# Stick-breaking attention: the gate projection dealt by whole groups of 24 matmuls in every second step

## The chip, the cores and the metric

One core of a Trainium2 chip. The metric is the device time of one execution of the whole program, in microseconds (us). The engines are TensorE (PE in the rows; PEld is its weight load), VectorE (DVE), ScalarE (ACT), GpSimd (POOL) and SyncE (SP), which issues the DMAs. Each engine works through its own instruction stream in order and waits on semaphores for the others.

## The reference

Two transformer-like blocks, batch 1, 1024 tokens, width 1024, float32. The first block runs a gated delta rule (branch a) and a stick-breaking attention (branch b) side by side and merges them through sigmoid gates; the second has latent and differential attention and a convolutional feed-forward. The edit concerns the stick-breaking attention and the gates:

```python
def _stick_breaking(q, k, v):              # 8 heads of 64
    scale = d ** -0.5
    for blk in range(s // SB_BLOCK):       # 8 tiles of 128 query rows
        z = einsum('bhqd,bhkd->bhqk', q[:, :, q0:end], k[:, :, :end]) * scale
        mask = kj < qi
        log_keep = where(mask, log_sigmoid(-z), 0.0)
        rest = cumsum(log_keep, axis=3, reverse=True) - log_keep
        a = where(mask, exp(log_sigmoid(z) + rest), 0.0)
        outs.append(einsum('bhqk,bhkd->bhqd', a, v[:, :, :end]))
...
gates = sigmoid(proj[..., B_Z1:G1] + b_gate)          # 2048 columns
merged = gates[..., :D_MODEL] * y_a + gates[..., D_MODEL:] * y_b
```

The matrix products with float32 inputs are done as three products of rounded parts (hi x hi, lo x hi, hi x lo).

## The kernel before

The program is a row of stages ("phases"). In each, several pieces of work ("stages" in the code) are written as generators, one for each engine, and a list, the plan, says which generator is advanced next. `run_stages` walks the same plan on every engine, so the plan fixes the order of the instructions in each of the five streams. The stage at hand is the phase `stick`, with three pieces in the plan: 0 is `StickAttention`, 1 is `GateProjection`, 2 is `BranchGates`.

**StickAttention** has 64 units: 8 tiles j of 128 query rows, by 8 heads h. A unit of tile j looks at j + 1 blocks of 128 keys. It runs as a software pipeline of 68 steps; step i holds, for unit i (tile i // 8, head i % 8):

- TensorE: in the first four steps of a tile four transposes of the next tile's prepared heads (`prep.turn`, L249) into a slot of `t`; the scores of unit i into `z` (L452 to L454); the products of unit i-3 with V into `o_acc` (`apply`, L476); the transposes of unit i-2's weights (`flip`, L463) into `t`. `t` has two slots, which head transposes and weight transposes take in turn.
- ScalarE: the high part of the transposed heads (`keep_hi`, L259), two sigmoids of the scores (`keep` L378, `chance` L381), in step 4 of a tile the squares for tile j + 2 (L213), then the copy of unit i-2's transposed weights out of the slot (L391).
- VectorE: the low part of the heads (`keep_lo`, L272 or L275), which frees their slot; the reversed scan of unit i (L426); in step 4 the sums for tile j + 2 (L219) and in step 7 their scaling (L239); the weights of unit i-1 (`weigh`, L402); and in step 2 of a tile `give` (L408), which multiplies the finished tile's `o_acc` into `stick_o`. The first products of a tile, in its step 3, wait for `give` (`pe.wait_ge(self.o_out, j)`), for they write `o_acc` anew.
- SyncE: loads of the prepared inputs and stores of `stick_o`.

**GateProjection** makes the gates' logits, transposed: 16 tiles of 128 gate columns, each in two halves of 512 tokens, that is 32 groups. A group is 24 matmuls of 128x512 (8 blocks of the inner dimension, three products each) into the one bank `g_acc`, and then one sigmoid by ScalarE (L567) and one store. `walk()` cuts each group in two parts of 12 matmuls, and `steps()` is 4 x 16 + 1 = 65. ScalarE and VectorE split the weights of the next tile into hi and lo (L554, L573) in the first part of a tile's second half; the first tile is split before the first part. SyncE stores the group before and loads weights for the next tile.

**BranchGates** takes eight steps a tile: a norm of branch a's output on GpSimd (L684 to L691, step 1), multiplications with the sigmoid gate (L696, L699, step 3), and the gate of branch b (L704, step 6), with loads and stores by SyncE.

The plan of the phase is `even_plan(68, 65)`: for each of the 68 steps it writes one step of StickAttention, one of BranchGates, and then as many of GateProjection as are due.

Of the kernel before, what the change touches and what calls it, by code (L numbers as in the profile page):

```python
# [710 lines left out]
def even_plan(first, second):  # L711


    plan, given = [], 0
    for i in range(first):
        plan += [0, 2]
        want = second * (i + 1) // first
        plan += [1] * (want - given)
        given = want
    return plan  # L720


# [3893 lines left out]
```

## Time and profile before

| | |
|---|---|
| median of 3 runs | 2792.08 us (2791.32 to 2796.21) |
| profiled execution, its time | 2794.54 us |
| profiled execution, its span | 2792.8 us |
| TensorE busy | 2614.5 us, 94% of the span |
| VectorE busy | 1263.7 us, 45% |
| ScalarE busy | 938.2 us, 34% |
| GpSimd busy | 357.3 us, 13% |
| mean granted TensorE clock | 0.967 of full speed |

The span is counted from the first to the last instruction on the core; the device time lies 1.7 us above it. Busy time says how long an engine had an instruction in hand. In rows of the timeline the first number is the start in us from the span's start, the second the duration in us, "x3" that three neighbours of the same line are merged, and a bracket at the end how long the engine sat idle before the row and who released it. Matmul durations overlap: the next one starts before the modelled end of the one before, so distances between starts are read, not durations.

### The profile page before, as it was taken

What the parts mean: (1) busy time and instruction counts of PE and PEld (TensorE: products, weight loads), DVE (VectorE), ACT (ScalarE), POOL (GpSimd) and SP (SyncE); (2) the same over time, 40 slices, a digit from 0 to 9 for tenths busy, and PEclk for the clock granted to TensorE, in tenths of its full rate; (3) what the DMA queues carried; (4) which work ended last, traced back from release to release, by engine and by line L of the source; (5) the groups of instructions that cost most, each with busy time, mean ns of one, the idle gap of its engine ahead of it and who ended that gap; (6) DMA issues with size and microseconds to landing.
All of it is one profiled execution on the core that took longest, in us unless ns stands there. A gap on an engine that the chain in (4) does not pass through costs nothing. (4 is left out here: it accounts for less than half of the span.)

```text
span 2792.8 us, 36573 instructions
## 1 busy us (share of the span) xinstructions
PE 2614.5 (94%) x14702; PEld 2246.8 (80%) x14702; DVE 1263.7 (45%) x1762; ACT 938.2 (34%) x1541; POOL 357.3 (13%) x450
## 2 busy tenths in 40 slices
PE   8969999997799998999996989979999999999999
PEld 6849999997688886888885777868888888878877
DVE  6523444442466754543225767554323332333452
ACT  4223222221455652122114767532111211222331
POOL 1002222220332310001012223011000000000000
PEclk9989999999799998999997999989999999999999
DMA  4222221112332215442343111063222222255532
GB/s 144 86 77 80 62 68 52 52 41 68 106 113 88 80 50 192 155 143 82 121 135 119 46 39 47 18 222 89 83 68 68 68 83 76 91 189 176 192 102 80
DMA packets 223712, 268.91 MB, mean 96 GB/s; under 512 B 55060, under 2 KB 154004, under 8 KB 223544
## 3 DMA queue, kind: packets, MB, share of 16 engines
q1 hardware_dynamic: 223544, 266.58, 30.0%
q8 instruction: 117, 1.92, 0.3%
q14 instruction: 51, 0.42, 0.0%
HBM read 187.21 MB, written 79.32 MB: 95 GB/s over the span
## 5 line engine op out<-in xcount | busy, mean ns | idle before, releaser
L3784 PE MATMUL ffn_up_acc<-mixed_hi,ffn_ring_hi 128*128 128x512 f32 x704 | 274.6, 390 | 2.5 <-DVE mixed_lo L2926 2.5
L3784 PE MATMUL ffn_up_acc<-mixed_hi,ffn_ring_lo 128*128 128x512 f32 x704 | 274.3, 390 | 0.0
L3784 PE MATMUL ffn_up_acc<-mixed_lo,ffn_ring_hi 128*128 128x512 f32 x704 | 274.2, 389 | 0.0
L1379 PE MATMUL delta_acc<-delta_w_hi,xn_hi 128*128 128x256 f32 x640 | 191.6, 299 | 2.9 <-DVE delta_w_lo L1333 2.9
L1381 PE MATMUL delta_acc<-delta_w_hi,xn_lo 128*128 128x256 f32 x640 | 181.3, 283 | 0.0
L1380 PE MATMUL delta_acc<-delta_w_lo,xn_hi 128*128 128x256 f32 x640 | 181.1, 283 | 0.0
L3784 PEld LDWEIGHTS ffn_up_acc<-mixed_hi,ffn_ring_hi 128*128 128x128 f32 x704 | 132.2, 188 | 30.0 <-issue 2.9
L3784 PEld LDWEIGHTS ffn_up_acc<-mixed_hi,ffn_ring_lo 128*128 128x128 f32 x704 | 132.2, 188 | 27.5
L3784 PEld LDWEIGHTS ffn_up_acc<-mixed_lo,ffn_ring_hi 128*128 128x128 f32 x704 | 132.3, 188 | 27.1
L4043 DVE TENSOR_TENSOR ffn_feed_lo<-ffn_feed_raw,ffn_feed_hi 128x1536 fp32r<-128x1536 f32 x44 | 77.4, 1759 | 146.2 <-ACT ffn_feed_hi L4035 146.2
L3754 DVE TENSOR_SCALAR ffn_conv<-ffn_padded,ffn_taps 128x1024 f32<-128x1024 f32 x22 | 16.6, 753 | 274.8 <-ACT ffn_padded L3735 274.8
L1379 PEld LDWEIGHTS delta_acc<-delta_w_hi,xn_hi 128*128 128x128 f32 x640 | 122.2, 191 | 8.9 <-issue 5.5
L426 DVE TENSOR_TENSOR_SCAN stick_keep<-stick_keep,stick_zero 128x127 f32<-128x127 f32 (+7 forms) x64 | 92.4, 1444 | 74.1 <-ACT stick_keep L378 73.4
L3735 ACT ACTIVATE ffn_padded<-ffn_up_acc 128x1024 f32<-128x1024 f32 x22 | 22.6, 1027 | 301.4 <-PE ffn_up_acc L3784 301.4
L1380 PEld LDWEIGHTS delta_acc<-delta_w_lo,xn_hi 128*128 128x128 f32 x640 | 122.2, 191 | 0.0
L1381 PEld LDWEIGHTS delta_acc<-delta_w_hi,xn_lo 128*128 128x128 f32 x640 | 121.9, 191 | 0.0
L4035 ACT ACTIVATE ffn_feed_hi<-ffn_feed_raw 128x1536 fp32r<-128x1536 f32 x44 | 65.4, 1487 | 158.9 <-PE ffn_up_acc L4111 158.9
L593 PE MATMUL stick_g_acc<-xn_hi,stick_g_hi 128*128 128x512 f32 x256 | 107.8, 421 | 9.3 <-DVE stick_g_lo L573 8.8
L4111 PE MATMUL ffn_up_acc<-ffn_feed_hi 128*128 128x512 f32 x352 | 108.7, 390 | 1.4 <-DVE ffn_emb L3897 1.4
L4111 PE MATMUL ffn_up_acc<-ffn_feed_hi,ffn_feed_lo 128*128 128x512 f32 x352 | 108.5, 390 | 0.0
L4111 PE MATMUL ffn_up_acc<-ffn_feed_lo,ffn_feed_hi 128*128 128x512 f32 x352 | 108.4, 390 | 0.0
L594 PE MATMUL stick_g_acc<-xn_lo,stick_g_hi 128*128 128x512 f32 x256 | 102.0, 399 | 0.0
(440 smaller groups left out, 6462.3 us busy)
## 6 DMA issues: line engine op xcount, KB each, us to landing
ffn_feed_raw<-in_w_down SPq DMA_DIRECT2D x44, 512.0 KB, 4.0
ffn_ring_raw<-in_w_gate SPq DMA_DIRECT2D x11, 1024.0 KB, 5.3
ffn_ring_raw<-in_w_up SPq DMA_DIRECT2D x11, 1024.0 KB, 5.8
scratch_act_t<-ffn_silu SPq DMA_DIRECT2D x22, 512.0 KB, 2.7
ffn_feed_raw<-scratch_act_t SPq DMA_DIRECT2D x44, 256.0 KB, 2.9
delta_w_raw<-in_w_in SPq DMA_DIRECT2D x20, 512.0 KB, 4.0
scratch_projected<-delta_out SPq DMA_DIRECT2D x80, 128.0 KB, 1.7
stick_g_raw<-in_w_in SPq DMA_DIRECT2D x16, 512.0 KB, 4.7
```

Source lines behind the costliest of these rows:

```text
L426: nc.vector.tensor_tensor_scan(back, back, self.zero[:].to_broadcast([P, n - 1]), 1.0, ALU.mult, ALU.add).then_inc(self.scanned, 1)
L593: nc.tensor.matmul(self.acc[:], w_hi, self.hi[:, k, cols], start=(k == 0), stop=False, skip_group_check=True)
L594: nc.tensor.matmul(self.acc[:], w_hi, self.lo[:, k, cols], start=False, stop=False, skip_group_check=True)
L1379: nc.tensor.matmul(acc, self.hi[:, k, tok], w_hi, start=(k == 0), stop=False, skip_group_check=True)
L1380: nc.tensor.matmul(acc, self.hi[:, k, tok], w_lo, start=False, stop=False, skip_group_check=True)
L1381: last = nc.tensor.matmul(acc, self.lo[:, k, tok], w_hi, start=False, stop=(k == self.kt - 1), skip_group_check=True)
L3735: nc.scalar.activation(self.padded[s][:, taps - 1:], self.acc[s][:, 0, :], ACT.Copy).then_inc(self.copied, 1)
L3754: nc.vector.tensor_scalar(self.conv[s][:], self.padded[s][:, 0:SEQ], self.taps_sb[:, f, 0:1], None, ALU.mult).then_inc(self.tapped, 1)
L3784: last = nc.tensor.matmul(self.acc[s][:, br, cols], weight[:, k, ch], part[:, k, cols], start=(k == 0 and first), stop=(k == 7 and weight ...
L4035: self.nc.scalar.activation(self.hi[s][:], self.raw[s][:], ACT.Copy).then_inc(self.hi_done[s], 1)
L4043: self.nc.vector.tensor_tensor(self.lo[s][:], self.raw[s][:], self.hi[s][:].bitcast(F32), ALU.subtract).then_inc(self.lo_done[s], 1)
L4111: last = nc.tensor.matmul(t.pairs[j][:, half, :], part, weight[:, HALF + half * HALF:HALF + (half + 1) * HALF], start=begins, stop=ends, s ...
```

## The change

`even_plan` gives the gate steps out only behind odd steps, and there an even number of them; the last step gets what is left. Everything else is as it was.

```diff
@@ -714,9 +714,10 @@
     plan, given = [], 0
     for i in range(first):
         plan += [0, 2]
-        want = second * (i + 1) // first
-        plan += [1] * (want - given)
-        given = want
+        if i % 2 or i == first - 1:
+            want = second * (i + 1) // first if i == first - 1 else second * (i + 1) // first // 2 * 2
+            plan += [1] * (want - given)
+            given = want
     return plan
```

## Rows read from the trace of the kernel before

**Rows 1.** TensorE by windows: length, busy (instructions), granted clock, DMA share, GB/s

```profile
727.00:1055.00 328.00, 324.60 (x1974) 1.00 0.28 86
1630.00:1640.00 10.00, 8.47 (x55) 1.00 0.23 62
1650.00:1660.00 10.00, 7.40 (x58) 0.92 0.01 2
```

**Rows 2.** Waits of TensorE, 727 to 1056: total us, times, longest

```profile
PE stick_o_acc L476 <- DVE stick_o L408: 2.4, 4, 1.1
PE stick_g_acc L593 <- ACT stick_gate L567: 0.4, 2, 0.3
```

**Rows 3.** Timeline of steps 21 to 23: start, us, engine, line, instruction, [idle before]

```profile
803.21 0.34 PE L452 MATMUL stick_z<-stick_prep_k,stick_prep_q_hi 128*128 128x384 f32 x1
...
807.42 0.34 PE L452 MATMUL stick_z<-stick_prep_k,stick_prep_q_hi 128*128 128x384 f32 x1
...
807.83 0.83 PE L476 MATMUL stick_o_acc<-stick_v,stick_weight_t 128*128 128x64 f32 x6
...
808.75 0.42 PE L452 MATMUL stick_z<-stick_prep_k,stick_prep_q_hi 128*128 128x384 f32 x1
...
809.03 0.49 ACT L391 ACTIVATE stick_weight_t<-stick_t 128x384 f32<-128x384 f32 x1
...
809.57 0.88 PE L476 MATMUL stick_o_acc<-stick_v,stick_weight_t 128*128 128x64 f32 x6 [0.17 <-ACT stick_weight_t L391]
```

**Rows 4.** Timeline of step 2 in tiles 1, 3 and 7

```profile
757.55 0.38 PE L476 MATMUL stick_o_acc<-stick_v,stick_weight_t 128*128 128x64 f32 x2
...
761.11 0.69 DVE L408 TENSOR_TENSOR stick_o<-stick_o,stick_o_acc 128x512 f32<-128x512 f32 x1
...
823.92 0.83 PE L476 MATMUL stick_o_acc<-stick_v,stick_weight_t 128*128 128x64 f32 x6
...
825.18 1.30 POOL L691 TENSOR_TENSOR stick_a_o<-stick_a_o,stick_a_gain 128x512 f32<-128x512 f32 x1
825.25 2.31 DVE L426 TENSOR_TENSOR_SCAN stick_keep<-stick_keep,stick_zero 128x511 f32<-128x511 f32 x1
...
827.48 1.70 DVE L402 TENSOR_TENSOR stick_chance<-stick_chance,stick_keep 128x511 f32<-128x511 f32 x1
...
829.21 0.69 DVE L408 TENSOR_TENSOR stick_o<-stick_o,stick_o_acc 128x512 f32<-128x512 f32 x1
...
830.04 1.08 PE L476 MATMUL stick_o_acc<-stick_v,stick_weight_t 128*128 128x64 f32 x8 [1.10 <-DVE stick_o L408]
...
1002.46 1.72 PE L476 MATMUL stick_o_acc<-stick_v,stick_weight_t 128*128 128x64 f32 x14
...
1007.94 0.69 DVE L408 TENSOR_TENSOR stick_o<-stick_o,stick_o_acc 128x512 f32<-128x512 f32 x1
```

**Rows 5.** Timeline of step 4 in tile 3

```profile
834.73 1.05 PE L476 MATMUL stick_o_acc<-stick_v,stick_weight_t 128*128 128x64 f32 x8
...
835.61 1.22 DVE L426 TENSOR_TENSOR_SCAN stick_keep<-stick_keep,stick_zero 128x511 f32<-128x511 f32 x1 [3.09 <-ACT stick_keep L378]
...
836.89 0.61 ACT L391 ACTIVATE stick_weight_t<-stick_t 128x512 f32<-128x512 f32 x1
...
838.18 0.68 DVE L402 TENSOR_TENSOR stick_chance<-stick_chance,stick_keep 128x511 f32<-128x511 f32 x1
```

**Rows 6.** Timeline of step 0 in tile 1

```profile
749.77 0.38 PE L476 MATMUL stick_o_acc<-stick_v,stick_weight_t 128*128 128x64 f32 x2
...
750.39 0.75 DVE L272 SCALAR_TENSOR_TENSOR stick_prep_q_lo<-stick_t,stick_prep_gain,stick_prep_q_hi 128x512 fp32r<-128x512 f32 x1 [0.17 <-ACT stick_prep_q_hi L259]
```

**Rows 7.** Timeline of the first gate split

```profile
720.00 1.85 DVE L573 TENSOR_TENSOR stick_g_lo<-stick_g_raw,stick_g_hi 128x1024 fp32r<-128x1024 f32 x1 [1.83 <-ACT stick_g_hi L554]
```

**Rows 8.** Timeline of step 64, near the stage's end

```profile
1041.78 1.04 PE L463 MATMUL stick_t<-ident,stick_chance 128*128 128x128 f32 x8
1042.43 1.08 ACT L391 ACTIVATE stick_weight_t<-stick_t 128x512 f32<-128x512 f32 x2 [4.33 <-PE stick_t L463]
```

## The prediction

> **What bounds the kernel now.** I read the page's slices first, then the stage that the edit orders (the attention stage with the stick-breaking heads, about 690 to 1060 us), by windows, by TensorE's waits, and then row by row in time. From 727 to 1055 us TensorE is busy 324.6 of 328 us at a granted clock of 1.00 [rows 1]. Its named waits there are 2.4 us for VectorE's `stick_o` in four places and 0.4 us for the gate's activation [rows 2]. So TensorE's own instruction stream is the stage. Neither side of the edit changes the number of matmuls, so nothing can be gained in the steady part beyond those few microseconds; what can be lost is the cover that the gate matmuls give to the chain ScalarE, VectorE, TensorE of the attention.
>
> How cover works shows where the plan before has a step without gate work, step 22 (tile 2, three key blocks). A step with 12 gate matmuls takes 807.42 - 803.21 = 4.21 us, step 22 only 808.75 - 807.42 = 1.33, so a half group is worth 2.88 us of TensorE. In step 23 the products with V start at 809.57 and not right behind the scores (about 809.24): they need ScalarE's copy of the transposed weights, 809.03 + 0.49 = 809.52 [rows 3]. One uncovered step cost 0.33 us, of which the trace names less.
>
> **What the change does.** `even_plan(68, 65)` gave one gate step (12 matmuls) to each stick step but 0, 22 and 45. Worked out by its formula, it now gives none to even steps and two (24 matmuls, 5.76 us) to steps 3, 5, ... 43 and 47 ... 65, none to 45, and the last three (a group and the final store) to step 67. No instruction is added or removed. In each pair (even a, odd a+1) TensorE runs scores, products and transposes of two steps in a row and only then 24 gate matmuls. Let S be the end of the scores of step a. Cover behind step a+1 is ample. What is late is what step a+1 needs from step a: the slot of `t` for its own head transposes, the copied weights of unit a-2 for the products, and VectorE's weights of unit a-1 for the transposes. For step 22 S is 807.83, and TensorE is ready for the next products 1.41 us later (809.24) at three key blocks: 808.75 - 807.83 = 0.92 for products and transposes, 0.31 a block, and 0.49 for the scores [rows 3]. I scale the first by the blocks, take 0.4 to 1.0 for the scores, and about 0.36 for head transposes where they lie between.
>
> *Pair (2,3) of tiles 1 to 7.* The products of step 3 (head 0) write `stick_o_acc` and wait until `give` has read it; `give` is VectorE's last instruction of step 2, behind keep_lo, the scan and the weights. From S to the end of `give` it is 761.80 - 757.55 = 4.25 us in tile 1, 829.90 - 823.92 = 5.98 in tile 3, and 1008.63 - 1002.46 = 6.17 in tile 7; the products follow 0.14 us behind [rows 4]. In tile 3 they started at 830.04 with 1.10 us of wait, so TensorE's work up to there was 5.02 us, 2.14 without the gate's 2.88. The wait becomes 5.98 + 0.14 - 2.14 = 4.0 us; in the same way, by the rate above, 3.1 in tile 1 and 2.9 in tile 7. Seven of 3.3 are 23 us: the upper bound. But scan and weights ran beside GpSimd's multiplies there: the scan took 2.31 us [rows 4], against 1.22 for the same shape in rows 5, and the weights 1.70 against 0.68. Without this tile 3 waits 1.9, and all seven about 14: the lower bound. GpSimd's work starts in step 1 and step 2 now comes 2.88 us later, but its last multiply needs step 2's sigmoid, so part of it still meets the scan. I take 20.
>
> The Trainium skill (GPSIMD Engine Reference, section 1, Specifications) says that GpSimd shares its SBUF interfaces with VectorE and contends with VectorE instructions that have two SBUF inputs. The scan of these rows agrees (2.31 beside a multiply, 1.22 alone); going by that rule for every one of the seven tiles would give the upper bound of 23.
>
> *Pair (4,5) of tiles 0 to 5.* In step 4 ScalarE squares the inputs of a later tile ahead of the copy, and VectorE sums them ahead of the weights. In tile 3, S = 834.73: the copy ends at 837.50, 2.8 later; the weights at 838.86, 4.1 later [rows 5]. TensorE is at the products at about 1.9 (four blocks and the scores), waits 0.9, spends 0.9 on them, and waits 0.5 more for the weights: 1.4. The same reading gives 2.2, 2.05, 1.7 (tiles 0 to 2) and 1.1, 0.6 (4, 5): 9.1, and with the gate's activation now ahead of every even step's first sigmoid in small tiles 9.5 us.
>
> *Pair (0,1) of tiles 1 to 6.* Step 1's head transposes need the slot of step 0's. In tile 1, S = 749.77 and keep_lo ends at 751.14 [rows 6]; with 0.05 of hand-over and about 0.15 for that activation it is 1.57 against 0.33 us of TensorE work: 1.2 us. In tiles 2 to 6 it is 0.8, 0.35, 0.05, 0.7, 0.65 (in the last two the slot is freed by the copy), with some 0.3 behind it: 4.1 us.
>
> *The rest.* Pairs with nothing extra, (6,7) mostly, by rows 3: 0.33 us at three blocks, more for shorter and less for longer units, 2.8 in all. Three steps in a row without cover (44 to 46): 0.3. At the end, step 65's products need the copy of unit 62: the transposes start at 1041.78 and the copies end at 1043.51 [rows 8]; eight transposes keep TensorE until about 1042.7: 0.9. At the start the gate's first split moves from step 1 to step 3 in ScalarE's and VectorE's order. It ended at 721.85 [rows 7]; behind steps 2 and 3 I put it near 724.5, some 2.7 later, while about 2.1 us of TensorE work of those steps moves into the wait: 0.6 (from -2 to +2). SP's loads keep their place, since nothing that SP waits for lies in steps 1 to 3; the gate's weight loads and stores are still issued a whole pair ahead of use.
>
> Sum of new waits: 20 + 9.5 + 4.1 + 2.8 + 0.3 + 0.9 + 0.6 = 38.2 us. What goes: the 2.8 us of rows 2, the 0.33 of step 22, and some 0.9 of like waits at step 45 and before head-0 transposes (steps 7, 15 ... now have double cover): 4.0. Net +34 us on the profiled execution (span 2792.8, 2794.5 with what lies around it), all of it in this stage; the same on the median of 2792.1: **2826 us**. The waits are not made good later, since TensorE has no slack in this stage, and the next stage starts from its last matmul: the last gate activation leads to the last two stores and those to the next stage's loads, in the same order as before.
>
> **Rivals.**
> *Only the bare uncovered step costs* (0.13). If `give` and the sums end by the time TensorE gets there, because ScalarE and VectorE enter step a with empty queues after 5.76 us of cover, each of the 31 pairs costs what step 22 did: 31 x 0.33 = 10, less 4: +6 to +12, 2801. Against it: rows 4 and 5 measure from S, behind which the chain starts afresh whatever the cover was.
> *The clock falls too* (0.07). TensorE now stops for 1 to 4 us in every pair. Rows 1 show 8.47 us busy of 10 at clock 1.00 with a wait in it, and 7.40 of 10 at 0.92; the worst pairs here, tiles 0 to 2, are busy some 75 to 80%. A group of 24 at half clock costs up to 5.8 us more; four to six of them make +57 to +69: 2855. The Trainium skill (TensorE: Matmul & The Clock Gate, "A second HAM failure mode") says that frequent short idling between groups can make the clock swing between its two levels; by that rule this rival would be the likeliest. The first of these rows speaks against it, the second for it.
> *Faster* (0.05). The long groups of 24 and the long weight-load wait at the head absorb the chains: the 4.0 us of old waits go, 2.1 us of steps 2 and 3 run while TensorE waited anyway, and the split isn't late. That is -6 us, 2786. It decides only if the chain from S is no longer than TensorE's work in the even step; at 4.25 against 1.3 us in tile 1 it is not.
> *No net change* (0.05): the waits come, but small, and match what is refunded: 2792, within 5.6 us.
>
> **Numbers.** The forecast has 0.70, its own range 2814 to 2838 (23 or 14 for `give`, half of the smaller terms either way). Slower in all: 0.70 + 0.13 + 0.07 = 0.90. A change is told from none at 0.2%, 5.6 us. The range reaches into the first rival below and to the upper bounds of all terms above: 2800 to 2843.
>
> **What would show it.** In the changed profile: TensorE's busy share of the stage falls from 99% to about 90%; a wait for `stick_o` in seven places, 2 to 4 us each; waits of the transposes for `stick_chance` and of the products for `stick_weight_t` in steps 5 of tiles 0 to 5; waits of step 1's head transposes; clock at 1.00; the stage's last gate activation some 34 us later than now; all stages behind as long as before. I would be wrong if the `stick_o` waits stay near 1 us, if GpSimd's multiplies have ended by every step 2, if the clock drops, or if TensorE's queue reaches past a waiting matmul.

## The result, and the profile after

The changed kernel takes 2841.68 us (median of 4 runs, 2836.43 to 2844.21) against 2791.7 (4 runs, 2790.81 to 2796.21): ratio 1.0174, 95% interval 1.0161 to 1.0187, so 1.7% slower, some 49 us. The forecast was 2826 in a range of 2800 to 2843; the direction and the place were right, the loss was nearly half as large again (49 us against 34).

The profiled execution took 2836.43 us with a span of 2834.7, 41.9 longer. I call the stretch from the attention's first sum on VectorE to the next stage's first load of `gated` the stage: it was 370.4 us (689.8 to 1060.2) and is 415.9 (689.0 to 1104.9), +45.5. Everything else went from 2422.4 to 2418.8. So the whole loss is in this stage.

TensorE by windows, as [rows 1] before (length, busy, granted clock, DMA share, GB/s), the second a stop in tile 2, the others in 1 us steps behind it:

```profile
727.00:1097.00 370.00, 336.80 (x1950) 0.97 0.25 76
804.00:806.00 2.00, 0.00 (x0) 1.00 0.68 203
...
807.00:808.00 1.00, 1.00 (x7) 0.58 0.48 178
808.00:809.00 1.00, 1.00 (x6) 0.50 0.97 182
...
810.00:811.00 1.00, 1.00 (x4) 0.72 0.29 98
811.00:812.00 1.00, 1.00 (x6) 1.00 0.00 0
```

Two things can be seen. TensorE is idle 33.2 us of 370, where it was 3.4 of 328. And the granted clock isn't 1.00 any more: behind the stop it goes to 0.50, the lower level of 1.2 GHz, with TensorE fully busy, and comes back near 811. Added up over 1 us windows as 2 x (1 - clock), the time at the lower level between 727 us and the last gate activation is 0 before and 22.1 us after.

TensorE's waits in the stage, as [rows 2] before:

```profile
PE stick_o_acc L476 <- DVE stick_o L408: 16.9, 7, 3.3
PE stick_o_acc L476 <- ACT stick_weight_t L391: 7.7, 11, 1.4
PE stick_t L463 <- DVE stick_chance L402: 2.5, 5, 0.9
PE stick_t L249 <- ACT stick_weight_t L391: 2.5, 5, 0.6
PE stick_t L249 <- DVE stick_prep_q_lo L272: 1.9, 3, 1.1
PE stick_t L249 <- DVE stick_prep_k L275: 1.5, 2, 1.0
```

Seven waits for `give` (VectorE L408), the copies (ScalarE L391), the weights (`stick_chance`, L402) and the slot of the head transposes (L249): the places that the forecast named. Tile 3, steps 2 and 3, answers to [rows 4]:

```profile
845.08 0.83 PE L476 MATMUL stick_o_acc<-stick_v,stick_weight_t 128*128 128x64 f32 x6
...
846.40 2.04 DVE L426 TENSOR_TENSOR_SCAN stick_keep<-stick_keep,stick_zero 128x511 f32<-128x511 f32 x1
...
847.70 1.80 POOL L699 TENSOR_TENSOR stick_a_o<-stick_a_o,stick_a_sig 128x512 f32<-128x512 f32 x1 [0.33 <-ACT stick_a_sig L657]
...
848.37 1.68 DVE L402 TENSOR_TENSOR stick_chance<-stick_chance,stick_keep 128x511 f32<-128x511 f32 x1
...
850.08 0.69 DVE L408 TENSOR_TENSOR stick_o<-stick_o,stick_o_acc 128x512 f32<-128x512 f32 x1
...
850.92 0.52 PE L476 MATMUL stick_o_acc<-stick_v,stick_weight_t 128*128 128x64 f32 x3 [3.31 <-DVE stick_o L408]
```

Step 2's products start at S = 845.08. Scan, weights and `give` follow one another without a gap, and end 5.69 us later (5.98 before); the products of step 3 wait 3.31 us for them (1.10 before). Scan and weights still run beside GpSimd's multiplies: 2.04 and 1.68 us.

### The profile page after: what moved, and what is told of

It reads as the page before. It is cut to its first block and busy times, and to the rows that moved or that the text cites. A ratio compares the mean times of both kernels' runs of the same rounds, so it can differ in the third digit from the quotient of the medians.

```text
span 2834.7 us, 36573 instructions
## 1 busy us (share of the span) xinstructions
PE 2625.7 (93%) x14702; PEld 2253.5 (79%) x14702; DVE 1258.6 (44%) x1762; ACT 936.4 (33%) x1541; POOL 349.7 (12%) x450
## 3 DMA queue, kind: packets, MB, share of 16 engines
q1 hardware_dynamic: 223544, 266.58, 29.7%
## 5 line engine op out<-in xcount | busy, mean ns | idle before, releaser
L3785 PEld LDWEIGHTS ffn_up_acc<-mixed_lo,ffn_ring_hi 128*128 128x128 f32 x704 | 132.7, 188 | 27.3
```

What stands on the lines that cost most here:

```text
L3785: last = nc.tensor.matmul(self.acc[s][:, br, cols], weight[:, k, ch], part[:, k, cols], start=(k == 0 and first), stop=(k == 7 and weight ...
```

## The experiments

The first column of the table is the ratio to the kernel before with its 95% interval. The others are from one profiled execution each: the stage's length less before's 370.4; TensorE's idle time and the time at the lower clock level, both from 727 us to the last gate activation. In e5 the last group comes some steps before the stage's end, so that its idle column lacks the drain, the steps 64 to 67 in which the pipeline empties (10.7 us up to 1066 us). The profiled execution is the shortest of its kernel in the change, e1, e3 and e6 and the longest in e2, e5 and e7, so the stage's column and the ratio can differ by some us.

| | ratio (95%) | stage, us | idle, us | lower clock, us |
|---|---|---|---|---|
| before | | 0 | 3.5 | 0 |
| the change | 1.0174 (1.0161 to 1.0187) | +45.5 | 33.2 | 22.1 |
| e1, step 2 alone | 1.0134 (1.0117 to 1.0150) | +38.3 | 24.5 | 34.2 |
| e2, step 4 alone | 1.0038 (1.0025 to 1.0051) | +11.6 | 13.0 | 0 |
| e3, steps 0 and 6 alone | 1.0048 (1.0034 to 1.0061) | +14.5 | 14.7 | 0 |
| e4, even steps | 1.0156 (1.0143 to 1.0169) | +44.3 | 27.3 | 38.3 |
| e5, steps 1, 2, 4, 7 | 1.0036 (1.0022 to 1.0050) | +12.0 | 9.8 | 0.9 |
| e6, change and fillers | 1.0131 (1.0114 to 1.0148) | +39.0 | 16.7 | 4.7 |
| e7, change, give first | 1.0097 (1.0083 to 1.0111) | +31.2 | 24.1 | 9.7 |
| e8, before, give first | 0.9989 (0.9980 to 0.9997) | -3.2 | 1.2 | 0 |
| e9, e5 with other last places | 1.0046 (1.0032 to 1.0060) | +13.2 | 11.5 | 0 |

Theory A is the forecast's mechanism with the clock added: a step pays for the chain that loses its cover, and where TensorE stops long the clock falls as well. Its rivals are C, all uncovered steps cost the same; D, groups of 24 matmuls in a row, or half of the steps without gate work, cost in themselves; and B, the clock costs nothing.

**One kind of step at a time (e1, e2, e3).**

```diff
         want = second * (i + 1) // first
+        if i % 8 == 2 and i > 8:          # e1
+        if i % 8 == 4 and i < 48:         # e2
+        if i % 8 in (0, 6) and i > 2:     # e3
+            want = given
         plan += [1] * (want - given)
```

Each kernel has one of the three conditions. That of e1 also meets step 66 of the drain, where its trace shows no wait.

e1 expected: 

> The plan of before, but the gate step of step 2 of tiles 1 to 7 is given behind step 3 instead (24 matmuls there). Theory A (each pair pays for the chain that it uncovers, and the clock falls where TensorE stops longest): the waits for stick_o rise from 2.4 to about 17 us in seven places, and in about five of them the granted clock falls for some 3.4 us, which costs 1.7 us each; +14.5 + 8.5 = about +23 us. Theory B (only the waits cost, the clock is a side effect): +14.5. Rival C (every uncovered step costs the same, what step 22 costs): seven times 0.33, +2.3 us, no more.

e2 expected: 

> The plan of before, but the gate step of step 4 of tiles 0 to 5 is given behind step 5. Theory A: the copy of the weights and the weights themselves come late behind the squares and sums; TensorE waits about 2.2, 1.9, 1.5, 1.1, 0.7, 0.6 = 8 us, and the clock falls at most once (tile 0): +8 to +10 us. Rival C: six times 0.33, +2 us.

e3 expected: 

> The plan of before, but the gate steps of steps 0 and 6 of each tile (from step 6 on) are given behind steps 1 and 7. Theory A: the head transposes of step 1 wait for their slot, 2.9 us over six tiles, the products of step 7 for the copy, about 1.1 us, less what waits before step 0's head transposes go; clock 1.00 throughout: +3 to +4 us. With e1 and e2 it should add up to the change, about +37 of its +50, the rest being the first two steps, the end and the clock. Rival C: fifteen times 0.33, +5 us.

Waits of TensorE in the stage, e1:

```profile
PE stick_o_acc L476 <- DVE stick_o L408: 17.6, 7, 3.6
...
PE stick_g_acc L593 <- ACT stick_gate L567: 3.7, 6, 0.9
```

e2:

```profile
PE stick_o_acc L476 <- ACT stick_weight_t L391: 5.2, 7, 1.0
PE stick_g_acc L593 <- ACT stick_gate L567: 2.8, 4, 0.9
...
PE stick_t L463 <- DVE stick_chance L402: 2.2, 4, 0.8
```

e3:

```profile
PE stick_g_acc L593 <- ACT stick_gate L567: 8.5, 11, 0.9
...
PE stick_t L249 <- DVE stick_prep_q_lo L272: 1.6, 3, 0.9
PE stick_o_acc L476 <- ACT stick_weight_t L391: 1.3, 4, 0.8
```

C falls: seven steps of kind 2 cost 37 us, six of kind 4 cost 11, fifteen of kinds 0 and 6 cost 13. e1 shows the `give` waits as expected (17.6 us in seven places), but cost 37 us and not 23. The clock was low for 34.2 us, twice what was expected, for it fell behind all seven; and idle time grew by 21.0 us where 14.5 were expected, with waits for the gate's sigmoid and for head transposes on top. The sum nearly closes: idle +21.0, half of 34.2 is 17.1, together 38.1 against the stage's 38.3. Half is what rows at either level give, roughly: in the changed kernel the starts of two gate matmuls lie 0.43 us apart at the lower level (725.14 and 725.56) and 0.23 at the upper (1099.50 and 1099.73).

All three hold a wait that the change has not: the first matmul of a group for the gate's sigmoid, 3.7, 2.8 and 8.5 us. I had not foreseen it, and it is why e3 missed its expectation of 3 to 4 us (e2, with 8 to 10 expected, came near). Less this wait e3's fifteen steps cost some 5 us, 0.35 each, which is what step 22 cost and what C had said for them; it is the steps of kinds 2 and 4 that C has wrong. Steps before the doubled one hand out one half group each, so 24 matmuls in a row can be the second half of one group and the first half of the next, with the sigmoid of 0.69 us between, and there is only the one bank `g_acc`. The change deals whole groups and has none. Less these waits (15.0, and 0.4 of before's in each) the three cost 61.4 - 13.8 = 47.6 us in all; the change costs 48.6. That the two agree to 1 us is partly luck, for the falls of the clock don't add.

**Whole groups behind even steps (e4).**

```diff
-        if i % 2 or i == first - 1:
+        if i % 2 == 0 or i == first - 1:
```

> Whole groups of 24 as in the change, but behind even steps. Theory A: what decides is which chain the uncovered (odd) step starts. The waits for stick_o go back to below 1 us and those behind squares and sums vanish; in their place the head transposes of step 0 wait for VectorE's scaling of step 7 (2.27 us long, ahead of it sigmoid and scan), some 2.5 to 3 us in each of seven tiles, +18 to +20, the slots in step 2 some 4, the rest 3; with the clock falling in up to seven places (1.7 us each) +30 to +38 us. Theory D (24 matmuls in a row are themselves what costs, or the longer idle of ScalarE): the same +50 as the change. Rival E (only step 2 and 4 are expensive): within 5 us of before.

Waits in e4:

```profile
PE stick_t L249 <- DVE stick_prep_xn L239: 17.0, 6, 3.0
PE stick_o_acc L476 <- ACT stick_weight_t L391: 4.3, 11, 0.8
```

The `stick_o` waits are gone from the list and those for `stick_prep_xn`, VectorE's scaling in step 7, are new: 17.0 us in six places, up to 3.0. Another chain gave the same price. The ratio can't be told from the change's, so e4 alone leaves D standing. Idle is less than in the change (27.3), the lower clock longer (38.3): half of it, 19.1, and 23.8 of added idle are 42.9 of the stage's +44.3. Rival E, that only steps 2 and 4 matter, falls, and 44 us is more than the 30 to 38 that I had expected, by the clock.

**Whole groups behind steps 1, 2, 4 and 7 (e5), and with other last places (e9).**

```diff
-        want = second * (i + 1) // first
+        due = sum(k % 8 in (1, 2, 4, 7) for k in range(1, i + 1))                                            # e5
+        due = sum(k % 8 in (1, 2, 4, 7) and k < 56 or k in (58, 62, 65, 66) for k in range(1, i + 1))        # e9
+        want = second if i == first - 1 else min(2 * due, second - 1)      # e5; in e9 2 * due, which never exceeds second - 1
         plan += [1] * (want - given)
```

e5 expected: 

> Whole groups of 24 as in the change, but behind steps 1, 2, 4 and 7 of each tile, so that give (step 2), squares and sums (step 4) and the scaling (step 7) are covered and the cheap steps 0, 3, 5 and 6 are not; steps 64 to 66 have no cover. Theory A: left are the slot of the head transposes (2.9 us), the copies behind steps 3, 5 and 6 (some 5 us) and the drain at the end (2.5), less 4 us of old waits: idle about 14 us against 33 in the change, no wait long enough for the clock to fall: +5 to +12 us. Theory D (groups of 24, or that half of the steps have no gate work, are what costs): near the change's +50.

e9 expected: 

> As e5, but the last four groups stand behind steps 58, 62, 65 and 66, so that the drain of the pipeline is covered; steps 59 to 61 and 63 and 64 of tile 7 are not, where eight key blocks keep TensorE long enough. Theory A: e5's stage ended 13.3 us later than before's; the three waits in the drain (1.5, 0.8, 0.8 as idle time before the copies and products, and the last product with nothing behind it) go, and the stage ends 7 to 9 us later than before's: +4 to +9 us. Theory D (a gap between e5 and before is due to groups of 24 in themselves): no better than e5, +10.

Waits in e5:

```profile
PE stick_o_acc L476 <- ACT stick_weight_t L391: 4.6, 13, 0.8
PE stick_t L463 <- DVE stick_chance L402: 3.4, 7, 0.9
...
PE stick_t L249 <- DVE stick_prep_q_lo L272: 1.9, 3, 1.1
PE stick_t L249 <- ACT stick_weight_t L391: 1.0, 2, 0.6
```

The same 32 groups of 24, half of the steps still without gate work, and a loss of 10 us in place of 49. D falls as the cause of the 49 us. No wait for `give`, sums or scaling is left, the longest of the rest is 1.1 us, and the clock stays (the 0.9 us in the table are at 727 us, the end of the low stretch with which the stage begins). e9 missed its expectation of 4 to 9 us with 13: the drain itself was covered, but steps 63 and 64, which now had no gate work, brought two waits of 0.8 us for the copies, and nothing was won. That is what D had said for e9, no better than e5, and a small D isn't excluded: of the stages' +12.0 and +13.2 us, idle time and clock explain about 7 and 8, and the other 5 are taken up behind the forecast's terms.

**What the clock costs (e6).**

```diff
             if 0 <= i - self.LAG - 1 < len(self.units):
+                gate, count = self.gate, 8 * (i % 8 == 3 and 8 < i < 64) + 4 * (i % 8 == 5 and i < 44)
+                if count:
+                    pe.wait_ge(gate.gated, (i - 3) // 2 - (i > 45))
+                    for _ in range(count):
+                        nc.tensor.matmul(gate.acc[:], c["ident_r"][:], gate.hi[:, 0, 0:HALF], start=True, stop=True,
+                                         skip_group_check=True)
                 apply(i - self.LAG - 1)
...
+                stick.gate = gate
```

> The change, with 8 matmuls of 128x512 that nothing uses put ahead of the products of step 3 (tiles 1 to 7) and 4 ahead of those of step 5 (tiles 0 to 4), where TensorE waits anyway. It leaves the waited-for instructions where they are. Theory A with the clock as a cost of its own: half-clock time of 22 us goes to about 0 and TensorE's idle time falls by some 16 us; the time falls by half of the half-clock time, 8 to 11 us, to about +40 us against before. Theory B (the clock costs nothing, because the half-clock stretches are refunded by later waits): the time stays at +50. If the fillers delay the products themselves, +51 to +55.

Waits in e6:

```profile
PE stick_o_acc L476 <- DVE stick_o L408: 4.8, 6, 1.5
PE stick_o_acc L476 <- ACT stick_weight_t L391: 3.1, 8, 0.8
```

With 76 matmuls more, some 18 us of TensorE work, the kernel is faster than the change: ratio 1.0131 with an interval that ends at 1.0148, where the change's begins at 1.0161; that is +37 us where about +40 was expected. TensorE's low-clock time goes from 22.1 to 4.7 us, half of the difference is 8.7, and the stage is 6.5 shorter; in tile 6, where the wait was 0.86 us, the eight fillers are longer than what they fill. B falls: the clock's share is a loss of its own. In tile 3 the clock fell even so (847 to 851 us), behind a wait of 1.47 us that the fillers had left.

**give ahead of the scan, in the change (e7) and in the kernel before (e8).**

```diff
+                u = i - self.LAG - 1
+                if 0 <= u and self.units[u][1] == H - 1:
+                    give(self.units[u][0])
                 dve.wait_ge(self.kept, i + 1)
                 back = self.keep[b][:, n - 1:0:-1]
...
-            if 0 <= u < len(self.units) and self.units[u][1] == H - 1:
+            if i >= len(self.units) and 0 <= u < len(self.units) and self.units[u][1] == H - 1:
                 give(self.units[u][0])
...
-        want = second * (i + 1) // first                                    # e8 only, in even_plan
+        want = second if i == first - 1 else i - (i >= 60) - (i >= 62)      # e8 only
```

e7 expected: 

> The change, with VectorE's give moved ahead of the scan in step 2 of each tile. Theory A (give is late because it stands behind scan and weights): the waits for stick_o fall from 16.9 to about 3 us; scan and weights come 0.6 to 1.2 us later, so step 3's transposes wait 0.5 to 2 us instead, 8 us in all; half the clock falls go: 12 to 20 us less than the change, +30 to +38 against before. Rival: the products wait for something else as late as give (copy, slot), and nothing is won.

e8 expected: 

> The plan of before with give ahead of the scan, and with the two stick steps without gate work moved from 22 and 45 to 60 and 62, where eight key blocks cover the copy. Theory A: 2.4 us of waits for stick_o and about 0.6 us at the two steps go: -1 to -3 us, which the measurement hardly tells from nothing. Rival: the scan that comes later costs as much elsewhere, 0 to +2 us.

Waits in e7, whose lines stand three further down (L463 is L466, L476 is L479):

```profile
PE stick_t L466 <- DVE stick_chance L402: 9.9, 12, 1.6
PE stick_o_acc L479 <- ACT stick_weight_t L391: 7.7, 11, 1.4
```

The 16.9 us of waits for `stick_o` are gone, while the transposes wait 9.9 us for the weights (2.5 in the change), for scan and weights now come later; low-clock time falls to 9.7. The result, +27 us, is 22 better than the change and a little better than the 30 to 38 expected: it was `give`'s place at the end of VectorE's step 2 that made step 2 the dearest. In the kernel before the same edit, with the two steps without gate work moved to 60 and 62 (tile 7, eight key blocks), leaves 1.2 us of idle in place of 3.5 and gives 0.9989 (0.9980 to 0.9997): some 3 us faster than before, as expected, and the fastest of all here. By the trace most of it is `give`: the four waits for it are gone and one of 0.35 us for the weights is new, while step 22's wait was 0.17; by time the two edits weren't told apart.

## Why the prediction was right, and where it was short

*What bounds the stage, and the sign.* Right: TensorE had 3.4 us of idle, nothing was to be won there, and covers were to be lost. e5, with the groups placed by the chains, loses 10 us.

*Pair (2,3), give, 20 us.* Right. In the change the waits for `give` are 16.9 us in seven places; in the same pairs the head transposes of step 3 wait first, 2.9 us in five places, which my sum from S held inside the 20. Together 19.8, by tile (1 to 7) 3.6, 3.4, 3.3, 3.2, 3.0, 1.2 and 2.2. That 20 was met so closely is partly luck, for the split by tile is another: the upper bound had 4.0 in tile 3 and 2.9 in tile 7. Between the two bounds (14 and 23) the meeting with GpSimd went as taken: beside the multiplies the scan took 2.04 us and the weights 1.68 in tile 3, against 1.22 and 0.68 in [rows 5]. In tile 6 the scan ran between two multiplies, and the wait for `give` was 0.86. What the meeting costs rests on these rows; no run takes the multiplies away.

*Pair (4,5), 9.5 us.* Measured by tile 2.2, 1.9, 1.5, 1.1, 0.7, 0.6, in all 8.0, against 2.2, 2.05, 1.7, 1.4, 1.1, 0.6. *Pair (0,1), 4.1:* 2.9. *The rest, 2.8:* 1.1 named by the trace; as in step 22 it names less than the rows show. *Steps 44 to 46, 0.3:* 0.28. *The end, 0.9:* 0.83. *The start, 0.6:* the first gate matmul comes at 724.12, not 721.90; counted from the stage's own start (689.03, not 689.81) that is 3.0 later, with about 2 us of TensorE work moved ahead of it, so some 1 us. All waits together are 33.2 us of idle against 3.5, +29.7; the forecast had +34.

*The clock.* Here the forecast fell short. "The clock falls too" stood beside the forecast as a rival with 0.07, so that it was no term of the sum, and was priced at four to six groups run wholly at the lower level. What happened is the forecast's waits and the clock: it fell behind the five stops of 2.5 to 3.3 us (tiles 1 to 5) and behind tile 0's 1.38 and 0.85 us within 2 us of each other, not behind the 2.18 us of tile 7 nor the 0.86 of tile 6; 22.1 us at the lower level, which cost half of it, 11. (Of the 22.1, 1.6 at 727 to 729 us are the end of the low stretch with which the stage begins.)

The rows that I weighed it by were windows of 10 us with 8.5 and 7.4 us busy, and I read them by their busy time alone. The second holds more when it is taken in steps of 1 us: TensorE stood still for 1.84 us up to 1657.27, and one us later, while it was busy, the granted clock went to 0.72 and then to 0.50, where it stayed to about 1665, through a second stop of 1.84 us before 1661.19. So the trace of the kernel before already held a fall of the clock behind a stop shorter than those that the forecast itself put into seven tiles. Seen so, there was reason to make the clock a term of the sum and not a rival with 0.07; its price of four to six groups (23 to 35 us) would have been too high, for it cost 11. The first window had stops of 0.39 and 1.13 us, at a clock of 1.00.

Of the page of the Trainium skill that I cited (TensorE: Matmul & The Clock Gate, "A second HAM failure mode") the trace shows the swing between the two levels. Here it came behind single long stops, or two stops close together, and not behind frequent short ones: e2, e3, e5 and e9 have about twenty waits each, of up to 1.1 us, and no fall behind any of them. In between it isn't settled: in e7, where no wait is longer than 1.62 us, the clock fell twice, behind 1.37 and 0.85 us in tile 0 and behind 1.04 us and a shorter one in tile 2, and not behind the 1.62; in e6 it fell behind 1.47.

*The rest, and the range.* The sum then reads +29.7 of idle and +11.0 of clock, 40.7 of the stage's +45.5. Counted over the whole stage up to the last gate activation's end it is the same: TensorE is idle 57.8 us against 29.3, and busy at the lower level for 24.2 us more, which makes 28.5 and 12.1, together 40.6. So the other 4.9 lie neither in idle time nor in the clock but inside TensorE's busy time, with 2016 matmuls both times; waits that hide behind the modelled ends of matmuls would be counted there. The same rest is 4.9 us in e5 and 5.1 in e9, and 1.5 in e1, which leaves only seven steps more without gate work. An estimate from step 22 would be enough for it: there the trace named 0.17 us of 0.33, and 0.16 for each of 31 uncovered steps is 5.0. No run tests it, and it is the part of rivals C and D that stays open.

That 2842 lies inside the stated range is partly luck. The upper end, 2843, was made of larger waits; the waits came out smaller than the sum had them, and the clock and this rest, for neither of which the sum had a term, filled the gap. Of the signs named beforehand, TensorE's busy share (91% of the window) and the places of the waits came as said; the last gate activation came 44.7 us later and not 34; and "if the clock drops", which stood among the signs of being wrong, came too.

The profiled run was the fastest of the four (2836.4 us; the others 2840 to 2844). Their mean granted clocks are 0.966, 0.965, 0.964 and 0.964 in the order of their times: 0.002 less over 2840 us is 11 us more at the lower level, 6 us of time. More falls of the clock in the other three would fit, but no profile of them was taken.

## What to carry to other kernels

Work dealt out as cover between the steps of a chain is worth what the step behind it would wait, and the steps differ: here taking 12 matmuls away cost 0 to 1 us behind most steps, 1 to 2 behind those with squares and sums (e2), and about 5, with the clock that fell after it, behind the one whose last VectorE instruction the next products wait for (37 us for seven in e1). Before covers are bunched, follow each kind of step from a common point to the last thing that the next step needs, on each engine in its program order; and if they must be bunched, put them where these chains are longest, and cut them at the boundaries of their own accumulation. When the sum leaves TensorE standing for some us at a stretch, look in the trace at hand for stops of that length, in steps of 1 us, and see whether the granted clock fell behind them; if it did, add half of the time at the lower level as a term of its own, not as a rival.

## What the runs showed of the hardware

Useless matmuls in a wait of 2.5 to 3.3 us made a kernel faster than the same kernel without them (1.0131 against 1.0174): 76 of them took about as much time as the idle time that went (16.5 us), and the time at the lower level fell from 22.1 to 4.7 us. Where waits were the same and long, the clock's falls differed from kernel to kernel: e1 and the change both wait about 17 us for `give` in seven places, but the change fell in five of these tiles and was low for 22.1 us in all, e1 fell in all seven and was low for 34.2. Nor does the length of the stop alone decide: the clock fell behind 1.79 us in e1 (tile 5) and not behind 2.18 us in the change (tile 7). What decides it in a given tile was not told apart.
